# Both condition products ahead of the turning, their weights ahead of the projection's, between two transformer blocks on one core

## The reference, cut to what matters

```python
x = x + _hier_moe(_rms(x, ffn_norm_g), ...)        # first block, 32 experts, two per token
x = _rms(x, final_norm_g)                          # end of the first block

mod = (silu(c) @ w_ada + b_ada).reshape(1, 6, 1024)     # second block: six vectors of 1024
sh1, sc1, g1, sh2, sc2, g2 = [mod[:, j, None, :] for j in range(6)]
u = modulate(x, sh1, sc1)                          # normalize(x) * (1 + sc1) + sh1
proj = u @ w_in                                    # 1024 x 2560: x_lru, y_lru, q, k, v
...                                                # recurrence, attention, w_out
x = layernorm(ALPHA * x + g1 * mix, ...)
ffn = hierarchical_moe(modulate(x, sh2, sc2), ...) # second 32 experts
x = layernorm(ALPHA * x + g2 * ffn, ...)
```

## Time and profile before

| | us |
|---|---|
| Median of 3 runs | 914.57 (913.44 to 915.78) |
| The profiled execution | 915.7 |
| its span in the trace | 913.8 |
| PE busy / DVE busy / ACT busy | 856.8 / 505.8 / 348.6 |
| Mean granted clock of TensorE | 0.992 of full speed |

### The profile page before, as it was taken

The page is one execution under the profiler, slowest core; times in us unless marked ns, Lnnn a source line. Parts: engine busy times, 40 slices in busy tenths (PEclk is TensorE's granted clock), DMA queues, the critical chain, the costliest instruction groups (busy, mean ns, idle before and its releaser), DMA issues.

```text
span 913.8 us, 14985 instructions
## 1 busy us (share of the span) xinstructions
PE 856.8 (94%) x5584; PEld 552.4 (60%) x5584; DVE 505.8 (55%) x1119; ACT 348.6 (38%) x686; POOL 22.3 (2%) x41
## 2 busy tenths in 40 slices
PE   8999999999999998998888899999899999999995
PEld 6778557987977533443333379876664555455552
DVE  5877668555456666433333486789764643333335
ACT  5674435455355322222222366754621111111113
POOL 1010111000000000000000000000000000000000
PEclk9999999999999999999999999999999999999998
DMA  9655894556626899999999997530769899999991
GB/s 356 253 196 223 320 382 190 184 184 232 257 112 258 330 409 362 427 426 425 426 426 425 422 370 294 215 155 1 292 231 369 338 406 423 425 425 425 425 418 55
DMA packets 29958, 285.35 MB, mean 312 GB/s; under 512 B 3113, under 2 KB 5577, under 8 KB 8913
## 3 DMA queue, kind: packets, MB, share of 16 engines
q1 hardware_dynamic: 26400, 278.25, 75.2%
q0 software_dynamic: 1136, 3.74, 1.3%
q10 hardware_dynamic: 2368, 2.64, 0.9%
HBM read 283.56 MB, written 1.06 MB: 311 GB/s over the span
## 4 chain that ended last, share of the span: by engine, by line
PE 65%; DMA 17%; DVE 11%; ACT 4%; issue 2%; SPq 1%; DVEq 0%; ACTq 0%
DMA ring<-in_experts 13%; PE bank L1162 11%; PE bank L743 8%; PE bank L1182 7%; PE bank L745 7%; PE bank L744 7%; PE bank L1210 5%; PE bank L1167 3%; DMA arena<-in_mem 2%; DVE ring_r L526 2%; PE bank L1174 2%; PE bank L1118 2%; DMA ring<-in_ada 1%; PE bank L720 1%; PE bank L1264 1%
## 5 line engine op out<-in xcount | busy, mean ns | idle before, releaser
L526 DVE TENSOR_TENSOR ring_r<-ring,ring_r 128x1024 fp32r<-128x1024 f32 (+1 forms) x84 | 99.4, 1212 | 65.9 <-ACT ring_r L519 65.7
L1162 PE MATMUL bank<-ring,arena 128*64 128x256 f32 x992 | 113.9, 382 | 1.0 <-DVE arena L2498 0.6
L519 ACT ACTIVATE ring_r<-ring 128x1024 fp32r<-128x1024 f32 (+1 forms) x84 | 85.0, 1046 | 68.1 <-PE bank L745 67.4
L743 PE MATMUL bank<-HT_r,ring_r 128*128 128x256 f32 x352 | 102.0, 290 | 1.3 <-DVE arena_r L2066 0.7
L745 PE MATMUL bank<-HT_r,ring_r 128*128 128x256 f32 x352 | 99.6, 283 | 0.0
L1182 PE MATMUL bank<-ring,arena 128*64 128x512 f32 (+1 forms) x488 | 91.7, 604 | 0.7 <-DVE arena L2575 0.7
L1162 PEld LDWEIGHTS bank<-ring,arena 128*64 128x64 f32 x992 | 69.8, 137 | 36.5 <-issue 6.4
L1777 ACT ACTIVATE arena<-bank 128x512 f32<-128x512 f32 (+1 forms) x64 | 31.4, 490 | 137.8 <-PE bank L1162 80.3
L744 PE MATMUL bank<-XN_r,ring_r 128*128 128x256 f32 x288 | 81.5, 283 | 0.0
L1167 PE MATMUL bank<-ring,arena 128*32 128x512 f32 x480 | 57.7, 597 | 22.5 <-DMA ring<-in_experts 22.0
L1210 PE MATMUL bank<-arena_r 64*128 64x512 f32 x496 | 74.1, 417 | 4.3 <-DVE arena_r L2555 3.8
(11 more groups left out here) (503 smaller groups left out, 1422.3 us busy)
## 6 DMA issues: line engine op xcount, KB each, us to landing
ring<-in_experts SPq DMA_DIRECT2D x61, 2048.0 KB, 15.3
ring<-in_experts SPq DMA_DIRECT2D x61, 1024.0 KB, 12.6
ring<-in_ada SPq DMA_DIRECT2D x12, 2048.0 KB, 11.4
ring<-in_win SPq DMA_DIRECT2D x5, 2048.0 KB, 15.1
ring<-in_hy SPq DMA_DIRECT2D x3, 2048.0 KB, 18.1
ring<-in_mk SPq DMA_DIRECT2D x2, 2048.0 KB, 11.0
ring<-in_mv SPq DMA_DIRECT2D x2, 2048.0 KB, 9.5
ring<-in_wo SPq DMA_DIRECT2D x2, 2048.0 KB, 8.7
```

What stands on the lines that cost most here:

```text
L519: nc.scalar.activation(R(h), w, ACT.Copy).then_inc(sem("w_high"), 1)
L526: nc.vector.tensor_tensor(R(w), w, R(h), ALU.subtract).then_inc(sem("w_low"), 1)
L743: mm(ps, R(ah), R(bh), start=first, stop=False)
L1162: last = mm(gu_bank[g * wide:(g + 1) * wide, 0:256], xw[:, k, :], w[k // 4][:, k % 4, g * 256:(g + 1) * 256], start=k == 0, stop=k == KD - 1)
```

## The change

It has three parts. `UNITS2` has `ada11` before `win0` instead of behind it. PE runs `ada(10)` and `ada(11)` one behind the other ahead of the turning, and the four constant matmuls of `occupy` are gone. The condition's bank is 7 instead of 1, and the first bank of `xl` is 1 instead of 7. ACT's, DVE's and POOL's programs are as they were, with line numbers lower by one.

```diff
--- before.py
+++ after.py
@@ -166,7 +166,7 @@
-UNITS2 = [(n, 4096) for n in ("ada10", "win0", "ada11", "win2", "win3", "win1", "win4", "wp0", "wp1")]
+UNITS2 = [(n, 4096) for n in ("ada10", "ada11", "win0", "win2", "win3", "win1", "win4", "wp0", "wp1")]
@@ -207,8 +207,8 @@
 STAGES += _moe_stages(1)
-STAGES += [("ada10", 1, (1,))]
-STAGES += [("uT", 4, (3, 4, 5, 6)), ("xl", 2, (7, 0)), ("adac11", 1, (2,)), ("aq", 2, (3, 4)),
+STAGES += [("ada10", 1, (7,))]
+STAGES += [("uT", 4, (3, 4, 5, 6)), ("xl", 2, (1, 0)), ("adac11", 1, (2,)), ("aq", 2, (3, 4)),
            ("ga", 2, (5, 6)), ("gx", 2, (7, 0)), ("ak", 2, (1, 2)), ("g1r", 2, (3, 4))]
@@ -1319,10 +1319,9 @@
             moe(1)
 
-            occupy("xl", 0, 4)
             ada(10)
+            ada(11)
             transposed("uT", XN, KD, "xn_u")
-            ada(11)
             channel_out("xl", ["win0"], HT, low_x, banks_of("uT"))
             ada_col(11)
```

## The result

The changed kernel takes 918.83 us (median of 16 runs, 916.51 to 923.25), the kernel before 915.17 us (16 runs, 913.15 to 918.24). The ratio is 1.0038, with a 95% interval from 1.0024 to 1.0051: 3.5 us more, between 2.2 and 4.7.

What follows compares the result with a forecast made beforehand. PE's start of xl, behind the third load and its product, was taken to bound the kernel. A late start of 2.55 us plus 1.7 for the clock made +4.25, so 918.8 us from a median of 914.57; range 916.3 to 920.8.

Steps and rivals of the forecast that it cites:

- The third place lands when it lands: Queue of loads between the blocks: whatever unit is third lands at 531.45, with issue and size, 2 MB, unchanged.
- ACT stands still for 3.4 us, and the modulation with it: ACT, ready at 528.05, waits for win0 until about 531.5; the modulation behind it starts at 533.6 instead of 530.20.
- `xl` starts 2.55 us later: Start of projection xl on PE: 535.9 against 533.33, 3.4 us of ACT's stall less a gain of 0.9 us.
- `ada(11)` inside PE's wait for DVE, ended by 528.1: Second condition product runs 526.2 to 528.1, ahead of the turning; by itself a gain of 0.9 us for xl.
- The fillers and the bank, 0 by themselves: Removing occupy's matmuls and moving the condition to bank 7, ahead of the first condition product, each gain 0.
- The clock, +1.7: A 5.1 us hole on PE ahead of xl lowers the clock for one 3.42 us stretch; lower bound 0.
- a half of a second is added: Around xl's start: half of a second low-clock stretch follows the first, for a clock cost of 2.5 us.
- half of what PE works in it: Price of a low-clock stretch around xl: 3.42 / 2 = 1.7 us if all of it falls on xl.
- Chunk 1 follows in the same distances: Within xl: the chunk after chunk 0 keeps its distances, DVE's low part of chunk 0 not being late; no added cost.
- the clock stays up: Rival: PE's hole ahead of xl doesn't lower the clock, leaving +2.55 us, 917.1; chance 0.13.
- The delay isn't taken up later: Attention stage after 590 keeps xl's delay; the rival that some 2 us vanish there gives 916.6, chance 0.08.
- The rule on queues that take turns: DMA ahead of the third landing: later bias_rows loads bring it up to 1 us forward, about +1.5; the forecast took nothing.

Runs made afterwards that it cites:

- e2: The kernel before with only the list of loads changed, ada11 second and win0 third; ratio 1.0046 (1.0031 to 1.0060) to the kernel before.
- e4: The changed kernel with ACT's high and DVE's low parts of win0's chunks 0 and 1 moved behind the modulation's first two quarters; 1.0014 on the kernel before.
- e1: The changed kernel with nine constant matmuls put on PE between the turning and xl; ratio 1.0032 (1.0017 to 1.0046) to the kernel before.
- e5: The kernel before with only the four constant matmuls of occupy taken out; ratio 1.0012 (0.9996 to 1.0029) to the kernel before.
- e6: The changed kernel with nine constant matmuls ahead of xl, and DVE's diag1 and reciprocal moved behind win0's low parts of chunks 2 and 3; 1.0024 on before.
- e3: The changed kernel with the list of loads of before, win0 second and ada11 third; ratio 1.0075 (1.0050 to 1.0101) to the kernel before.
- e7: The kernel before with ada11 loaded seventh, its product ahead of the attention loop in its own bank, and diag1 later; ratio 1.0012 (0.9995 to 1.0028).
- e8: The kernel before with ada11 seventh, its product ahead of attention, diag1 later, three constant matmuls ahead of xl, column sums in bank 3; 913.44 us, ratio 0.9982.

## Why the prediction was right, point by point

The measured 918.83 is the 918.8 that was forecast, and that closeness is partly luck: the median of before moved from 914.57 to 915.17 with more runs. The fair comparison is the difference, forecast 4.25 us, measured 3.5 (2.2 to 4.7), and 4.7 in the trace.

- *The third place lands when it lands.* Right: 12.68 us from issue against 12.67.
- *ACT stands still for 3.4 us, and the modulation with it.* Right: 3.32 us. e2 and e4 show that this is the mechanism and not what stood beside it.
- *`xl` starts 2.55 us later.* Right: 2.58, and 2.58 again in e1 and e2. Two terms of the sum were off and cancel, which is luck: from ACT's first high part to the modulation it took 2.00 us and not 2.15, and from DVE's split to PE's start 0.26 and not 0.05.
- *`ada(11)` inside PE's wait for DVE, ended by 528.1.* Right: it waited 1.66 us for its load and ended at D + 6.2, ahead of the turning. It brought nothing, since PE was not what was awaited.
- *The fillers and the bank, 0 by themselves.* Right for the start of `xl` (e5: 11.32 against 11.33), and 0.37 us short at its end. That they keep the clock was named as possible, and shows in e5. The bank had no run of its own; e2, with the banks of before, starts `xl` as late as after.
- *The clock, +1.7.* The mechanism was right and the size too small: 2.10 in the trace, the whole of what `xl` takes longer in after (13.80 us against 11.70). The level stayed low for 6.83 us and not 3.42, of which 5.04 lay on `xl`; the case "a half of a second is added", priced at 2.5, was the one that came. The step "half of what PE works in it" overrates a given stretch, since the stream runs at 0.213 us per matmul against 0.12: 5.04 us cost 2.2 and not 2.5. The two errors go against each other, and the forecast was nearer than its working.
- *"Chunk 1 follows in the same distances".* Right for after, by the low clock: PE waits for nothing within `xl`. At full clock it doesn't hold. `xl` starting right behind its inputs meets DVE at `diag1`, 0.68 us (e1: 12.38 us for `xl` against 11.70; e6: 11.59 with `diag1` moved). Had the rival "the clock stays up" come true, it would have been +3.3 and not +2.55.
- *The delay isn't taken up later.* Right in the trace: 4.68 at the end of `xl`, 4.8 at the last execution of line 1201.
- *The rule on queues that take turns.* The two loads of `bias_rows` were issued at 529.91 in after, when `win0` had landed, and the landing was no earlier for it (12.68 us against 12.67). In e4 ACT issued them 3 us ahead of the landing, and ACT could start on `win0` at D + 9.47, where it is D + 9.46 in after. The Trainium skill, "DMA: Bandwidth & Descriptors", section "Queues, rings and completion order", says that each DMA engine goes round the queues that have work for it, packet by packet. What that does to a landing no run here shows, since ACT's queue moved next to nothing before the third landing in any of these three traces.

What stays open: the share of the clock in the times. The traces give 2.1 us against before and 1.42 against e1, and but the interval of the ratio of after overlaps with those of e1 and e6.

## What to carry to other kernels

An order of loads is priced at every engine that waits for them in order, and at what stands behind the waiting instruction: PE's product became free of its wait, and ACT's modulation, which had nothing to do with either load, paid 2.6 us. Where a queue of loads is full, something must be third, so put there what nobody wants before the bottleneck engine has idle time of its own. A hole of some microseconds on PE costs beyond its length, and a few matmuls on constant data in it can keep the clock at no cost: with nine of them `xl` starts at D + 13.91 in e1, as in after, and ends 1.42 us earlier.

## What the runs showed of the hardware that was not expected

Half the granted clock isn't half the pace everywhere. The projection's matmuls (128x256, rounded operands, each with its own weights) went from 0.12 to 0.213 us, 1.8 times; the condition product of 16 records went from 1.92 to 3.64 us in e3, 1.9 times.

The level also falls at places that no kernel here changed. In the traces it was down for 3.41 us around 131 us in before, around 351 us in e1, e2, e3, e5, e6, e7 and e8, around 617 us in e3, and around 650 us in all but e2, e3, e5 and e8. And line 1201, ahead of which nothing was changed, started between 520.44 and 522.40 in the ten traces. The two latest of them (before, 522.00, and e6, 522.40) had a fall early on, around 131 and 10.5 us, but e5 with 521.87 had only the one around 351 that earlier starters had too, so that the falls are not the whole cause. What the rest is stays open; it is why distances from a common instruction were compared here and not spans.
